# Two projection pieces interleaved with the norm, value banks emptied earlier, SBUF buffers shifted

## What is computed

```python
h = rmsnorm(x, norm_mix[l])
proj = h @ w_in[l]
qa, ka, va, qb, kb, vb = jnp.split(proj, splits, axis=-1)
gates = jax.nn.sigmoid(h @ w_branch_gate[l] + b_branch_gate[l])
```

## Time and profile before

| | |
|---|---|
| median of 3 runs | 2596.25 us (2594.32 to 2597.88) |
| profiled execution | 2592.82 us |
| its span | 2590.9 us |
| TensorE matmul busy | 2336.4 us, 90% |
| VectorE busy | 1297.8 us, 50% |
| ScalarE busy | 1024.0 us, 40% |
| GpSimd busy | 848.0 us, 33% |

### The profile page before, as it was taken

How to read it: one execution, slowest core, us unless ns; L and a number is a source line. 1 busy time by engine, 2 the same in 40 slices (tenths; PEclk the granted TensorE clock), 3 DMA queues, 4 the chain that set the end, 5 groups by cost and what they waited for, 6 DMA issues and landing times. The chain is left out here.

```text
span 2590.9 us, 36773 instructions
## 1 busy us (share of the span) xinstructions
PE 2336.4 (90%) x12238; PEld 1986.4 (77%) x12239; DVE 1297.8 (50%) x1949; ACT 1024.0 (40%) x1778; POOL 848.0 (33%) x799
## 2 busy tenths in 40 slices
PE   5999998999997888896999999379999999999990
PEld 4888887788886788885899998268888888888870
DVE  6012222211110777776433333657757757798774
ACT  6111111211111677774312221146646545666653
POOL 7365545530000111111322221134433434454451
PEclk9999999999998999998999999589999999999995
DMA  4247766632213667555544432378977979899977
GB/s 164 90 146 233 253 196 179 195 122 73 73 65 130 215 187 201 160 142 159 183 154 145 150 127 104 117 244 298 315 235 256 323 220 315 275 372 332 309 258 275
DMA packets 234881, 517.34 MB, mean 200 GB/s; under 512 B 24368, under 2 KB 90032, under 8 KB 233648
## 3 DMA queue, kind: packets, MB, share of 16 engines
q1 hardware_dynamic: 158528, 340.18, 37.9%
q0 software_dynamic: 32352, 95.18, 14.9%
q10 hardware_dynamic: 43920, 80.95, 8.7%
HBM read 384.56 MB, written 131.66 MB: 199 GB/s over the span
## 5 line engine op out<-in xcount | busy, mean ns | idle before, releaser
L400 DVE TENSOR_TENSOR pj_w_lo<-pj_w_raw,pj_w_hi 128x1024 fp32r<-128x1024 f32 x38 | 50.7, 1334 | 572.2 <-ACT pj_w_hi L289 572.2
L289 ACT ACTIVATE pj_w_hi<-pj_w_raw 128x1024 fp32r<-128x1024 f32 x38 | 40.2, 1059 | 586.9 <-PE pj_bank L464 517.6
L464 PE MATMUL pj_bank<-pj_hT_hi,pj_w_hi 128*128 128x512 f32 x960 | 258.5, 391 | 7.8 <-DVE pj_f_lo L417 5.7
L464 PE MATMUL pj_bank<-pj_hT_lo,pj_w_hi 128*128 128x512 f32 x960 | 258.2, 391 | 0.0
L464 PE MATMUL pj_bank<-pj_hT_hi,pj_w_lo 128*128 128x512 f32 x960 | 256.9, 389 | 0.0
L1948 POOL TENSOR_TENSOR ex_wd_lo<-weights_raw_d,ex_wd_hi 128x1024 fp32r<-128x1024 f32 x64 | 192.2, 3026 | 130.6 <-ACT ex_wd_hi L1976 130.6
L464 PEld LDWEIGHTS pj_bank<-pj_hT_hi,pj_w_hi 128*128 128x128 f32 x960 | 181.0, 189 | 46.0 <-issue 8.5
L464 PEld LDWEIGHTS pj_bank<-pj_hT_lo,pj_w_hi 128*128 128x128 f32 x960 | 181.3, 189 | 37.9
L464 PEld LDWEIGHTS pj_bank<-pj_hT_hi,pj_w_lo 128*128 128x128 f32 x960 | 180.7, 188 | 37.7
L2030 DVE TENSOR_TENSOR ex_wd_lo<-weights_raw_d,ex_wd_hi 128x1024 fp32r<-128x1024 f32 x64 | 164.6, 2611 | 10.9 <-ACT ex_wd_hi L1976 10.9
L1539 PE MATMUL mg_y_ps<-mg_aT_hi,mg_w_hi 128*128 128x256 f32 x512 | 148.3, 290 | 11.3 <-DVE mg_gated L1450 8.0
(11 more groups left out here) (278 smaller groups left out, 5831.5 us busy)
## 6 DMA issues: line engine op xcount, KB each, us to landing
weights_raw_g<-in_w_exp_gate_dram SPq DMA_DIRECT2D x128, 512.0 KB, 8.4
weights_raw_u<-in_w_exp_up_dram SPq DMA_DIRECT2D x128, 512.0 KB
weights_raw_d<-in_w_exp_down_dram SPq DMA_DIRECT2D x128, 512.0 KB
pj_w_raw<-in_w_feat_dram SPq DMA_DIRECT2D x38, 512.0 KB, 4.8
scratch_gates<-pj_f_hi ACTq DMA_DIRECT2D x32, 512.0 KB, 5.0
mg_g_in<-scratch_gates SPq DMA_DIRECT2D x128, 128.0 KB, 3.1
pj_x_in<-in_x_dram SPq DMA_DIRECT2D x16, 512.0 KB, 3.5
scratch_qk<-pj_f_hi ACTq DMA_DIRECT2D x16, 512.0 KB, 7.0
```

The costliest lines, as they stand in the source:

```text
L289: act.activation(w_hi[n % 2][:], w_raw[n % 2][:], ACT.Copy).then_inc(whi_done, 1)
L400: dve.tensor_tensor(w_lo[n % 2][:], w_raw[n % 2][:], w_hi[n % 2][:], ALU.subtract).then_inc(wlo_done, 1)
L464: last = pe.matmul(eight[4 * p + b][:], w[p][:, k * P:(k + 1) * P], h[:, k, b * NB:(b + 1) * NB], start=(k == 0 and n == 0), stop=(k == KD ...
```

## The change

Pieces 0 and 1 are taken out of the piece loop of TensorE and run as 16 chunks of 12 matmuls (half of k, one block of 512 tokens), one behind each tile's transposes from tile 5 on, five behind the last tile. They use banks 4 to 7; the transposes now have two pairs of banks instead of four. ScalarE copies a chunk's bank every second tile; piece 1 goes to the `f_lo` buffers, and the four stores of both are issued by SP ahead of weight load 4. Weights 0 and 1 are scaled, copied and split in rounds 0 to 4. Rows of tiles 0, 2 and 4 are scaled by VectorE instead of GpSimd. The table with the root is loaded ahead of the first square, and roots follow their tile at once. In the value steps both ScalarE and VectorE empty the banks before they copy and split the next weight. At last, 160 bytes per partition of fill are added in front of the weight buffers of the later stages, and two one-column tensors of the experts move from the middle to the end.

```diff
-SCALE_AT, SPLIT_AT, LOW_AT = (5, 8), (6, 9), (7, 10)
+SCALE_AT, SPLIT_AT, LOW_AT = (0, 2), (1, 3), (2, 4)
+ROWS_ON_DVE = (0, 2, 4)
+FIRST_CHUNK = 5
+EARLY = 2
+EARLY_ORDER = [(p, b) for b in range(SEQ // NB) for p in range(EARLY)]
+EARLY_CHUNKS = [(p, b, part) for p, b in EARLY_ORDER for part in range(2)]
...
+            def store_early(p, half):
+                sp.wait_ge(plain_out, 4 * half + 3 + p)
+                sp.dma_start(feat[p][:, half * HALF:(half + 1) * HALF], early_buffers(f_hi, f_lo, p)[half][:].bitcast(F32)
+                             ).then_inc((hi_stored, lo_stored)[p][half], 16)
             for n in range(2, len(PIECES)):
+                if n == 4:
+                    for half in range(2):
+                        for p in range(EARLY):
+                            store_early(p, half)
...
-            for t in range(NT):
+            for t in (t for t in range(NT) if t not in ROWS_ON_DVE):
...
-                                   eight[2 * (t % 4) + b][:].rearrange("p (k t) -> p k t", k=4), ACT.Copy).then_inc(hi_done, 1)
+                                   eight[2 * (t % 2) + b][:].rearrange("p (k t) -> p k t", k=4), ACT.Copy).then_inc(hi_done, 1)
...
+            act.wait_ge(warm, 1)
+            act.activation(stat[0][:, 2:3], stat[0][:, 7:8], ACT.Sqrt)
...
             for n, (s, c) in enumerate(PIECES):
+                if n == last_piece(s) and KINDS[s] == TOKENS:
+                    evacuate_tokens(s)
+                if s == EARLY - 1:
+                    evacuate_early(*EARLY_ORDER[-1])
                 if n + 2 < len(PIECES):
                     split_weights(n + 2)
...
+            def scale_rows(t):
+                dve.wait_ge(x_ready[t % X_BUFS], t // X_BUFS * 16 + 16)
+                dve.tensor_scalar(x_in[t % X_BUFS][:], x_in[t % X_BUFS][:], stat[t % X_BUFS][:, 4:5], None,
+                                  ALU.mult).then_inc(h_dve, 1)
...
+            def early_chunk(p, b, part):
+                pe.wait_ge(tr_read, 2 * BLOCK_TILES * (b + 1) + 4)
+                pe.wait_ge(wlo_done, p + 1)
+                if b >= 4 // EARLY:
+                    pe.wait_ge(plain_out, EARLY * b + p - 3)
+                for k in range(4 * part, 4 * part + 4):
+                    for n, (w, h) in enumerate(((w_hi, hT_hi), (w_hi, hT_lo), (w_lo, hT_hi))):
+                        last = pe.matmul(eight[4 + (EARLY * b + p) % 4][:], w[p][:, k * P:(k + 1) * P],
+                                         h[:, k, b * NB:(b + 1) * NB],
+                                         start=(k == 0 and n == 0), stop=(k == KD - 1 and n == 2))
...
-            run(0, 2, None, 0)
...
+ROUTES_FILL = 40
...
+        self.fill = st.sb("fill", [P, ROUTES_FILL])
...
         idt = st.sb("idt", [P, P])
-        rows = st.sb("rows", [P, 1], U32)
-        targets = st.sb("targets", [P, 1], U32)
         x_in = st.sb("x_in", [P, D])
...
         y = st.sb("y", [P, D])
+        rows = st.sb("rows", [P, 1], U32)
+        targets = st.sb("targets", [P, 1], U32)
```

More of the change, by code:

```diff
@@ L150, in stores_from, with early_buffers @@
     queries = min(max(s - A_TILES, 0), QK_TILES // 2)
-    return 16 * (sum(per[kind] for kind in KINDS[:s]) + queries)
+    swapped = (1 if low else -1) if s > 1 else 0
+    return 16 * (sum(per[kind] for kind in KINDS[:s]) + queries + swapped)
+def early_buffers(f_hi, f_lo, p):
+    return (f_hi, f_lo)[p]
 def project(nc, x, norm_mix, w_feat, gate_bias, rope_cos, rope_sin, ident, feat, rot_q, rot_k, qk, q_swap, v_b, gates):
@@ L235, in _ @@
                 for half in range(2):
-                    pool.wait_ge(hi_stored[half], 16 * (r + 1))
+                    pool.wait_ge((lo_stored if r == 1 else hi_stored)[half], 16 * max(r, 1))
                 for c in range(SEQ // NB):
@@ L349, in evacuate_tokens, with evacuate_early @@
                                       buffer[:].bitcast(F32).rearrange("p (h c) -> p h c", h=8)).then_inc(stored, 16)
+            def evacuate_early(p, b):
+                if b < SEQ // NB - 1:
+                    act.wait_ge(early_done, EARLY_ORDER.index((p, b)) + 1)
+                else:
+                    act.wait_ge(mm_done, p + 1)
+                act.activation(early_buffers(f_hi, f_lo, p)[b // 2][:, b % 2 * NB:(b % 2 + 1) * NB].bitcast(F32),
+                               eight[4 + (EARLY * b + p) % 4][:], ACT.Copy).then_inc(plain_out, 1)
+            act.wait_ge(warm, 1)
+            act.activation(stat[0][:, 2:3], stat[0][:, 7:8], ACT.Sqrt)
             for t in range(3):
                 square(t)
-                if t > 0:
-                    root(act, stat[t - 1], t - 1, mean_done, root_done)
-            root(act, stat[2], 2, mean_done, root_done)
+                root(act, stat[t], t, mean_done, root_done)
+            early_at = {FIRST_CHUNK + 2 * i + 2: pb for i, pb in enumerate(EARLY_ORDER)}
             for t in range(NT):
@@ L363, in _ @@
                     split_weights(SPLIT_AT.index(t))
+                if t in early_at:
+                    evacuate_early(*early_at[t])
+            for p, b in EARLY_ORDER[(NT - FIRST_CHUNK - 1) // 2:-1]:
+                evacuate_early(p, b)
             act.wait_ge(const_in, 32)
             for n, (s, c) in enumerate(PIECES):
+                if n == last_piece(s) and KINDS[s] == TOKENS:
+                    evacuate_tokens(s)
+                if s == EARLY - 1:
+                    evacuate_early(*EARLY_ORDER[-1])
                 if n + 2 < len(PIECES):
                     split_weights(n + 2)
[L368 to L373, removed]
+                if n == last_piece(s) and KINDS[s] != TOKENS and s >= EARLY:
+                    evacuate(s)
+                    store(s)
             for half in range(2):
@@ L437, in _ @@
                     scale_weights(n + 2)
+                if n == last_piece(s) and KINDS[s] == TOKENS:
+                    evacuate_tokens(s)
+                if n + 2 < len(PIECES):
                     split_weights(n + 2)
@@ L440, in _ @@
                     evacuate(s)
-                if n == last_piece(s) and KINDS[s] == TOKENS:
-                    evacuate_tokens(s)
         @block.tensor
         def _(pe):
-            pe.sem_inc(tr_read, 8)
+            def early_chunk(p, b, part):
[8 more added lines that the diff above has]
+                                         start=(k == 0 and n == 0), stop=(k == KD - 1 and n == 2))
+                if part == 1:
+                    last.then_inc(early_done if b < SEQ // NB - 1 else mm_done, 1)
+            pe.sem_inc(tr_read, 4)
             pe.wait_ge(idt_in, 16)
             for t in range(NT):
-                pe.wait_ge(h_done, t + 1)
+                if t in ROWS_ON_DVE:
+                    pe.wait_ge(h_dve, ROWS_ON_DVE.index(t) + 1)
+                else:
+                    pe.wait_ge(h_done, t + 1 - sum(u < t for u in ROWS_ON_DVE))
                 pe.wait_ge(tr_read, 2 * t + 2)
                 for k in range(KD):
-                    last = pe.transpose(eight[2 * (t % 4) + k // 4][:, (k % 4) * P:(k % 4 + 1) * P],
+                    last = pe.transpose(eight[2 * (t % 2) + k // 4][:, (k % 4) * P:(k % 4 + 1) * P],
                                         x_in[t % X_BUFS][:, k * P:(k + 1) * P], idt[:])
                 last.then_inc(tr_done, 1)
-            pe.wait_ge(tr_read, 2 * NT + 8)
+                if t >= FIRST_CHUNK:
+                    early_chunk(*EARLY_CHUNKS[t - FIRST_CHUNK])
+            for chunk in EARLY_CHUNKS[NT - FIRST_CHUNK:]:
+                early_chunk(*chunk)
+            pe.wait_ge(tr_read, 2 * NT + 4)
             def features(p):
```

18 lines of the change are left out of this document (13 added, 5 removed).

## The result

| | before | after |
|---|---|---|
| median | 2595.74 us (2594.32 to 2597.88, 4 runs) | 2535.49 us (2532.84 to 2538.77, 4 runs) |
| profiled execution, its span | 2592.82, 2590.9 us | 2534.02, 2532.3 us |

What follows compares the result with a forecast made beforehand. TensorE was taken as the bound, waiting at the projection's norm and value banks and always busy in the experts. 19 + 17 + 18 = 54 us off 2592.8 is 2538.8, with 3.4 for the median 2542; range 2533 to 2566.

Steps and rivals of the forecast that it cites:

- Part 1: Norm at the projection's start: 192 matmuls moved between the tiles' transposes use TensorE's idle time; 19 us, ends 12 and 23.
- fourth copy: ScalarE's copy of the fourth weight, released by the end of piece 1; forecast at 87 us instead of 106.2.
- Part 2: Value steps of the projection: banks emptied ahead of weight copies and splits; 17 of 17.7 us, ends 10 and 18.
- The new wait: Value steps: banks 4 to 7 wait for stores, the next weight's copy stands behind bank 7; 17 of 17.7 us kept.
- My low end: Value steps: gain only 10 us if each store takes 11 us and a new 3 us stall comes at both places.
- Part 3: Experts: buffers moved so operands start alike modulo 512 bytes, 6.7 ns a matmul; 18 us, ends 0 and 22.
- The first rival: Experts: SBUF addresses don't matter, so moving the buffers gives nothing; 2560 us, chance 0.31.
- VectorE's bound in the norm: Norm: VectorE's chains slip, tile 5 at 36 us, later tiles over 3.7 apart, gain there 10; 2551, chance 0.08.
- the clock (2605): Tiles 5 to 15: TensorE's full clock isn't granted while transposes and chunks take turns; 2605 us, chance 0.03.

Runs made afterwards that it cites:

- the kernel with later weights: Changed kernel with the first two weights scaled in rounds 2 and 5, copied and split in 3 and 6; ratio to the kernel before 0.9756.
- part 2 alone: Kernel before with only the value banks emptied ahead of the next weight's copy and split; ratio to the kernel before 0.9932.
- the reordered kernel: Changed kernel with constants awaited later, weights scaled in rounds 1 and 4, tile 5's rows on VectorE, first chunk behind tile 4; ratio to the kernel before 0.9746.
- the kernel with fillers: The reordered kernel plus 16 and 14 unused identity transposes behind tiles 3 and 4; 2531.74 us, ratio to the kernel before 0.9752.

## Why the prediction was right

**Part 1: 21.6 us, forecast 19.** The path was as laid out and came a little sooner at each step: tile 0 at 7.71 (8.0), tile 3 at 20.49 (21.0), tile 5 at 28.20 (29.4), tile 6 at 34.02 (35.8), 3.62 us a tile (3.7), fourth copy at 84.57 (87). Mis-sized: the rows on VectorE, taken at 1.22 us by the two-input neighbour, cost 0.75, and 1.36 only for tile 4, beside GpSimd's tile 3; VectorE's wait for ScalarE's weight copy did not come about. Those two are most of the 1.2 us at tile 5. The chunk starts 1.62 us behind the tile's first transpose; I had taken the length of the group, 1.97, for a distance. The clock rose inside chunk 0, at its seventh matmul near 32.5, against 35. That two weights pulled forward hold tile 5 up was the claim that spoke against the change, and the kernel with later weights bears it out.

**Part 2: 17.5 us, forecast 17.** The new wait was where I put it: banks 4 to 7 at the stores, which landed faster than the 7.0 of the earlier trace rows (5.0 and 5.8 us at the median between 368 and 400 us), and the next weight's copy behind bank 7. TensorE waited 0.2 us. My low end, slow stores and a stall of some 3 us left over, is what the profile of part 2 alone shows at one of the two places, with a term that I had at nothing: the issue of the last two stores held ScalarE for 3.10 us.

**Part 3: 15.0 us in the profile, 16.6 to 17.7 by the medians, forecast 18.** The mechanism was right, but that the size came near is in part luck: its working was wrong in two terms that pull against each other. For experts with a single tile I counted 0.3 of the 0.48 us a step, because VectorE is busy 49.4 of 50 us there. All 44 later steps are 18.11 us long before and 17.73 after, and VectorE shows 50.00 of 50 us in the window above, at the shorter step: that busy share was no bound. And I gave each of the 72 matmuls of a step the full 6.7 ns, 0.48 us; a step gained 0.38. The gates, which follow on the down product without a break, gain the full 0.16 us (5.37 to 5.21 over 23 distances). The up and down products stand behind transposes, and there the first distances lie between 224 and 236 ns whatever the starts. 44 x 0.38 = 16.7; the stage shows 15.0, as its first step was 0.3 us longer and its end, from the last tile's transposes on, 16.2 us for 14.8. There TensorE waits 1.86 us for VectorE in both kernels; in the changed one the clock fell behind that wait (timeline of the last down product, first of the changed kernel, then of the kernel before):

```profile
2459.18 0.50 PE L2172 MATMUL ex_y_ps<-ex_wd_hi,ex_aT_hi 128*128 128x512 f32 x1 [1.86 <-DVE ex_aT_lo L2112]
...
2460.27 0.63 PE L2172 MATMUL ex_y_ps<-ex_wd_hi,ex_aT_hi 128*128 128x512 f32 x1
```

```profile
2518.33 0.50 PE L2096 MATMUL ex_y_ps<-ex_wd_hi,ex_aT_hi 128*128 128x512 f32 x1 [1.86 <-DVE ex_aT_lo L2036]
...
2519.14 0.39 PE L2096 MATMUL ex_y_ps<-ex_wd_hi,ex_aT_hi 128*128 128x512 f32 x1
```

Seven matmuls are 0.43 us apart in the one and none in the other. This too is chance of the execution, and not the change: of the fourteen profiles of this study, all with that wait of 1.86 us, five have seven or eight such matmuls there and an end of 16.1 to 16.4 us (the changed kernel both times, and three kernels with unlike starts), and nine have none and 14.5 to 14.8. Without it the stage would have gained some 16.6, the worth of part 3 in the medians.

The first rival, that addresses don't matter, was priced at 2560 and given 0.31. The Trainium skill ("Advanced Engine Details and Errata", SBUF Cachelines) has lines of 16 bytes. That their width settles nothing for two operands against each other these runs show: 32 bytes, two whole lines, cost 6.2 ns a matmul (down product, 233.3 for 227.1). VectorE's bound in the norm (2551) and the clock (2605) did not come. Of the clock, what came is what the sum had in it: chunk 0 took 4.2 us, forecast 4.4, where it takes 2.85 at the full clock.

**The rest.** 21.6 + 17.5 + 15.0 = 54.1 is the forecast sum, by luck as exact as that: part 1 was 2.6 us under, part 3 in the profile 3 over. The other 4.5 of the 58.6 us lie where nothing was changed, 2.0 in attend and 2.5 in pauses and the end. Over all traces of this study attend took 346.4 to 351.3 us and merge 432.2 to 435.9, with no order by the kernels' edits, so I give them no cause.

## What to carry to other kernels

Fill an engine's idle time with work that is due later, but count what is pulled forward with it: here two weights' scaling held up the tile that the filling starts from, and in the traces another order of VectorE's program and of the first chunk brought the fourth copy 3 us forward. Look at the distance from matmul to matmul, not at its busy share: where the same shape is spaced wider in one stage, compare the starts of its two operands before anything else. A busy share near one beside an engine that is never late is no bound.

## What the runs showed of the hardware

- The distance of float32 matmuls of 512 columns depends on where stationary and moving operand start in SBUF against each other: 226.7 ns alike, 227.2 with 256 bytes between them, 232 to 234 with 32 to 128. Why is open.
- Transposes of 128 x 128 stand 213 ns apart at TensorE's 1.2 GHz level and 109 at 2.4 GHz, so they show the clock where the profile's page has no record of it. Transposes alone raised it: among three tiles from 12.60 on, with a pause of 0.49 us, in the reordered kernel (third tile 1.07 us for eight), and with the first fillers in the kernel with fillers, whose third tile still took 1.94. Sixteen tiles of the kernel before, with pauses of 0.85 to 1.27 us between them, never raised it (1.97 each).
- Behind a pause of 2.82 us the clock was back at half (1.94 us for eight); behind one of 2.75 us, in the kernel with later weights, eight transposes still took 1.23, and the fall came in the chunk behind them. Behind the pause of 1.86 us at the end of the experts five of fourteen executions ran at half speed for seven or eight matmuls and nine did not.
- VectorE and GpSimd slow each other where both read two operands from SBUF: 2.31 for 1.22 us and 2.26 for 1.28. The Trainium skill ("SBUF — State Buffer", SBUF: two separate sides) has one port pair that the two take in turn, also for two-input instructions of VectorE; these rows agree. With one input each it went either way: in the changed kernel VectorE's row scaling took 1.36 for 0.75 (19.62) while GpSimd's kept its 2.84, in the reordered one GpSimd's took 3.29 (from 9.26) and VectorE's kept its 0.75 (10.91).
